# Last loop body of a mixture-of-experts kernel written out, with the last gate ahead of its predecessor's down

## The chip, the cores and the metric

The kernel runs on one core of one Trainium2 chip. The metric is the device time of one execution in microseconds; the median of three runs counts.

## What is computed

One inference step of a hybrid decoder with one layer: a mixing block (short convolution and a gated recurrence), then a mixture of experts over 320 tokens (256 new ones and 8 x 8 sampled ones), then a final norm. The change lies in the mixture of experts, where each token takes the best 4 of 32 experts:

```
for e in range(N_EXPERTS):                       # 32
    a = minimum(t @ w_gate[e] + b_gate[e], 7.0)
    u = clip(t @ w_up[e] + b_up[e], -7.0, 7.0)
    hid = (u + 1.0) * a * sigmoid(1.702 * a)
    y = y + combine[:, e:e+1] * (hid @ w_down[e] + b_down[e])
```

Every weight matrix is 1024 x 1024 in float32, 4 MB; 32 experts have 96 of them, 403 MB.

## The kernel before

**Slots.** In a round each expert takes up to 64 of its tokens. `gather(m)` picks their rows on TensorE with a matrix `P` of zeros and ones (the rows as three bfloat16 parts, L1299 and L1302), ScalarE copies them (`keep_rows`, L597), TensorE transposes them (`turn`, L1370) and VectorE writes the operand `xgT` (`gathered`, L962). `turn_gates` (L1364) makes the scatter matrix `PT`. After down, the result is split into three bfloat16 parts (`split_rows`: L625 and L627 on ScalarE, L980 and L983 on VectorE) and `scatter` (L1382) spreads them back over the tokens in three blocks; VectorE weighs each block and adds it to `x` (`add_rows`, L974).

**Products.** `product(mat, bank, lhs, e, it, j, between, operand)` computes one of gate (0), up (1), down (2): a bias row (L1391), then eight k steps of two halves (L1409; one half is two instructions in float32). After each second k it counts one slot as used (`wUsed`) and calls an entry of `between`.

**Ring.** Weights live in a ring of 16 slots of 1 MB, four matrices deep. SyncE issues the loads on one queue, each when the slots it overwrites are used. The loop's first bodies load whole matrices (L282); the last `FINE` = 2 bodies load halves of 2 MB (`load_half`, L287), and the last down ends in two pieces of 1 MB (`load_quarter`, L292). TensorE waits for the first half on `ringIn`, for the second on `lateIn` at k = 4, and for the last quarter of the last down on `endIn` at k = 6.

**Loop.** All engines run `Fori(0, BODIES)`: 8 bodies of 4 experts, 12 matrices each. For expert e TensorE does: gate of e, with the three scatters of e-1 between its k steps; up of e; `gather` of e+1; transposes of hidden (L1451), which ScalarE copies (L621) for down; `turn_gates` and `turn` of e+1; down of e. VectorE turns gate's result into `gt` (L1011, L1014, with ScalarE's sigmoid L617) and up's into `hid` (L1016, L1020). GpSimd writes `eh`, the row that selects expert e+1's bias (`pick`, L429). In the last expert the same instructions prepare expert 32, which doesn't exist. After the loop the last rows are scattered (L1479), added (L1047), normed (L637, L644, L1042) and stored.

All later rounds, for experts with more than 64 tokens, run only where there are any; here there are none.

Of the kernel before, what the change touches and what calls it, by code (L numbers as in the profile page):

```python
# [5 lines left out]
def hybrid_shortconv_hgrn2_moe_step(nc, A):  # L6
# [15 lines left out]
    E = 32  # L22
# [20 lines left out]
    FIRST = 4  # L43

# [34 lines left out]
    with ctx:  # L79
# [100 lines left out]
        endIn = sem("end_in")  # L180
# [70 lines left out]
        def credit(eng, *sems):  # L251
            for s in sems:
                eng.sem_inc(s, START)

# [24 lines left out]
        def _(sp):  # L279
# [64 lines left out]
            sp.sem_inc(endIn, 16)  # L344

            def body(first, it, halves=False, ends=False):
                for i in range(MPB):
                    s, e, m = (L_EXP + 4 * i) % NR, it * PER_BODY + i // 3, i % 3
                    used = lambda n: (first + 4 * (i - 4) + n) + it * (LPE * PER_BODY) + START
                    if halves:  # L350
                        sp.wait_ge(wUsed, used(2))
                        load_half(e, m, s, 0, ringIn[s])
                        if ends and i == MPB - 1:
                            sp.wait_ge(wUsed, used(3))
                            load_quarter(e, m, s, 2, lateIn[s // 4])
                            sp.wait_ge(wUsed, used(4))
# [11 lines left out]
                if not ends:  # L368
                    sp.sem_inc(endIn, 16)
# [27 lines left out]
        def _(pool):  # L397
# [34 lines left out]
            def one_round(r):  # L432
                pool.wait_ge(ehDone, r * (E + 1) + START)
                pool.wait_ge(wUsed, r * (LPE * E) + START)
                pick(slice(0, 1), 0)
                with pool.Fori(0, BODIES) as it:
                    for j in range(PER_BODY):
                        pool.wait_ge(wUsed, r * (LPE * E) + (it * (LPE * PER_BODY) + LPE * j) + START)
                        pick(bass.ds(it * PER_BODY + (j + 1), 1), (j + 1) % 2)

# [6 lines left out]
        def _(act):  # L447
# [142 lines left out]
            def one_round(r):  # L590
# [20 lines left out]
                with act.Fori(0, BODIES) as it:  # L611
                    for j in range(PER_BODY):
                        e = e0 + (it * PER_BODY + j)
                        m = p0 + (it * PER_BODY + (j + 1))
                        act.wait_ge(aDone, e + 1 + START)
                        act.wait_ge(hidDone, e + START)
                        act.activation(gs, ga, ACT.Sigmoid, scale=ALPHA).then_inc(sigDone, 1)  # L617
                        keep_rows(m)
                        act.wait_ge(hidTMM, e + 1 + START)
                        act.wait_ge(wUsed, e * LPE + START)  # L620
                        act.activation(hidT, ps[:, 4, :], ACT.Copy).then_inc(hidTOut, 1)  # L621
                        keep_slots(m, e * 3 + 3, (j + 1) % 2)
                        act.wait_ge(wUsed, e * LPE + LPE + START)
                        act.wait_ge(scatMM, e * 3 + 3 + START)
                        act.activation(ysb[0], ps[:, 2, :], ACT.Copy).then_inc(yHigh, 1)  # L625
                        act.wait_ge(yRest, e + 1 + START)
                        act.activation(ysb[1], yrest, ACT.Copy).then_inc(yMid, 1)  # L627
# [20 lines left out]
        def _(dve):  # L648
# [295 lines left out]
            def one_round(r):  # L944
# [22 lines left out]
                def add_rows(m0, e, par):  # L967

                    dve.wait_ge(gatesDone, m0 + START)
                    for b in range(3):  # L970
# [33 lines left out]
                with dve.Fori(0, BODIES) as it:  # L1004
                    for j in range(PER_BODY):
                        e = e0 + (it * PER_BODY + j)
                        m = p0 + (it * PER_BODY + (j + 1))
                        prepare(m, bass.ds(it * PER_BODY + (j + 1), 1))
                        add_rows(p0 + (it * PER_BODY + j), e, (j + 1) % 2)
                        dve.wait_ge(wUsed, e * LPE + 4 + START)  # L1010
                        TS(ga, ps[:, 0, :], LIMIT, None, ALU.min).then_inc(aDone, 1)  # L1011
                        dve.wait_ge(aDone, e + 1 + START)
                        dve.wait_ge(sigDone, e + 1 + START)
                        TT(gt, ga, gs, ALU.mult).then_inc(tDone, 1)  # L1014
                        dve.wait_ge(wUsed, e * LPE + 8 + START)
                        TS(gu, ps[:, 1, :], LIMIT, -LIMIT, ALU.min, ALU.max).then_inc(uDone, 1)  # L1016
                        dve.wait_ge(tDone, e + 1 + START)
                        dve.wait_ge(uDone, e + 1 + START)
                        dve.wait_ge(hidTMM, e + START)
                        STT(hid, gu, 1.0, gt, ALU.add, ALU.mult).then_inc(hidDone, 1)  # L1020
                        dve.wait_ge(accDone, e * 3 + 3 + START)
                        keep_gates(m, bass.ds(it * PER_BODY + (j + 1), 1), (j + 1) % 2)
                        gathered(m)
                        split_rows(e)
# [29 lines left out]
        def _(pe):  # L1054
# [292 lines left out]
            def one_round(r):  # L1347
                p0, e0 = r * (E + 1), r * E

                def gather(m):  # L1350

                    pe.wait_ge(prep, m + 1 + START)
                    pe.wait_ge(xgTOut, m + START)
                    if not isinstance(m, int):
# [31 lines left out]
                def product(mat, bank, lhs, e, it, j, between=(), operand=None):  # L1386
# [6 lines left out]
                    if operand:  # L1393
                        pe.wait_ge(*operand)
                    for k in range(KT):
                        n = LPE * j + 4 * mat + k // 2
                        s = (L_EXP + n) % NR
                        i = 3 * j + mat
# [6 lines left out]
                        if k == 6 and i == MPB - 1:  # L1405
                            pe.wait_ge(endIn, (r * BODIES + it) * 16 + 16)
# [21 lines left out]
                with pe.Fori(0, BODIES) as it:  # L1428
                    for j in range(PER_BODY):
                        e = e0 + (it * PER_BODY + j)  # L1430
                        m0 = p0 + (it * PER_BODY + j)
                        m = p0 + (it * PER_BODY + (j + 1))

                        def scatter_before(b, e=e, m0=m0, j=j):
                            if b == 0:
                                pe.wait_ge(yLow, e + START)
                                pe.wait_ge(yMid, e + START)
                                pe.wait_ge(gtOut, m0 + START)
                            scatter(b, e, (j + 1) % 2)

                        pe.wait_ge(ehDone, m + START)
                        pe.wait_ge(xgTOut, m + START)
                        pe.wait_ge(aDone, e + START)
                        product(0, 0, half_c(xgT), e, it, j, [lambda: None] + [lambda b=b: scatter_before(b) for b in range(3)])
                        pe.wait_ge(uDone, e + START)
                        product(1, 1, half_c(xgT), e, it, j)
                        gather(m)
                        pe.wait_ge(hidDone, e + 1 + START)
                        pe.wait_ge(hidTOut, e + START)
                        for c in range(4):  # L1450
                            ins = TR(ps[:, 4, 128 * c:128 * c + 128], fourth(hid, c), ident)  # L1451
                        ins.then_inc(hidTMM, 1)
                        turn_gates(m)
                        turn(m)
                        pe.wait_ge(yRest, e + START)
                        product(2, 2, half_c(hidT), e, it, j, operand=(hidTOut, e + 1 + START))
# [72 lines left out]
```

## Time and profile before

| | us |
|---|---|
| median of three runs | 1144.34 |
| lowest, highest | 1143.99, 1145.71 |
| the profiled execution | 1145.68 |
| its span, first to last instruction | 1143.9 |
| TensorE busy | 1107.1 (97%) |
| VectorE busy | 399.2 (35%) |
| ScalarE busy | 163.1 (14%) |
| mean DMA rate over the span | 378 GB/s |

The profile is of one execution, with times in microseconds from the span's start. Ends of matmuls are modelled, so that a busy TensorE isn't TensorE at its peak. "Idle before" an instruction is put down to what ended it. SPq, DVEq and the like are the queues in which an engine's instructions are issued. PE is TensorE's matmul, PEld its weight load, DVE VectorE, ACT ScalarE, POOL GpSimd, SP SyncE.

### The profile page before, as it was taken

The page shows a single profiled execution, that of the slowest core. Times are in us where ns is not written, and L with a number is a line of the kernel's source. Part 1 is how long each engine was busy: PE and PEld are TensorE (multiplying, and loading weights), DVE is VectorE, ACT ScalarE, POOL GpSimd, SP SyncE. Part 2 cuts the span into 40 slices and gives each one's busy share as a digit, 9 for nine tenths or more (in the row PEclk, how much of TensorE's full clock was granted, in tenths as well). Part 3 has the DMA queues.
Part 4 walks back from the last instruction along what each step waited for, and adds up shares of the span by engine and source line. Part 5 has one row for each costly group of instructions (what it writes and reads, how often), then busy time and mean ns, then how long its engine had stood idle before and what let it go on. Part 6 is the DMA issues. An engine that isn't in the chain of part 4 may idle for free.

```text
span 1143.9 us, 15163 instructions
## 1 busy us (share of the span) xinstructions
PE 1107.1 (97%) x6046; PEld 462.5 (40%) x6046; DVE 399.2 (35%) x711; ACT 163.1 (14%) x286; POOL 23.3 (2%) x51
## 2 busy tenths in 40 slices
PE   8999999999999999999999999999999999999996
PEld 5786764333333333333333333333333333333332
DVE  4155285633333333333332333322233332333333
ACT  3100114311111111111111011111111111111112
POOL 0002000000000000000000000000000000000000
PEclk9999999999999999999999999999999999999998
DMA  9970317799999999999999999999999999999993
GB/s 317 334 220 1 148 64 312 265 398 429 423 430 434 431 432 433 432 432 430 433 430 433 429 435 429 434 434 430 433 429 430 428 428 426 430 430 426 429 429 150
DMA packets 38990, 432.31 MB, mean 378 GB/s; under 512 B 2927, under 2 KB 18099, under 8 KB 22197
## 3 DMA queue, kind: packets, MB, share of 16 engines
q1 hardware_dynamic: 37312, 428.13, 89.9%
q0 software_dynamic: 848, 3.03, 0.7%
q10 hardware_dynamic: 805, 0.82, 0.2%
q8 instruction: 15, 0.25, 0.1%
q14 instruction: 10, 0.08, 0.0%
HBM read 428.26 MB, written 3.71 MB: 378 GB/s over the span
## 4 chain that ended last, share of the span: by engine, by line
PE 69%; DMA 28%; DVE 1%; ACT 0%; issue 0%; SPq 0%; DVEq 0%
PE ps L1409 39%; DMA ring<-in_w_gate 22%; PE ps L1117 9%; DMA ring<-in_w_up 6%; PE ps L1382 4%; PE ps L1234 3%; PE ps L1299 3%; PE ps L1391 2%; PE ps L1302 1%; PE ps L1370 1%; PE ps L1451 1%; PE ps L1107 1%; PE ps L1144 1%; PE ps L1364 1%; DMA consts<-in_consts 0%; PE ps L1111 0%
## 5 line engine op out<-in xcount | busy, mean ns | idle before, releaser
L1409 PE MATMUL ps<-ring,R 128*64 128x512 f32 x3072 | 691.4, 595 | 19.8 <-DMA ring<-in_w_gate 15.7
L1409 PEld LDWEIGHTS ps<-ring,R 128*64 128x64 f32 x3072 | 209.1, 137 | 421.1 <-issue 375.1
L974 DVE SCALAR_TENSOR_TENSOR x<-ps,gates,x 128x1024 f32<-128x1024 f32 (+1 forms) x96 | 106.2, 1106 | 136.9 <-PE ps L1382 136.9
L1117 PE MATMUL ps<-R,ring 128*128 128x320 f32 x384 | 107.3, 435 | 0.6 <-DVE R L687 0.6
L980 DVE TENSOR_TENSOR R<-ps,R 128x512 f32<-128x512 f32 x32 | 22.1, 692 | 228.9 <-ACT R L625 228.9
L1117 PEld LDWEIGHTS ps<-R,ring 128*128 128x128 f32 x384 | 71.8, 190 | 31.2 <-issue 1.8
L1382 PE MATMUL ps<-R 64*128 64x512 bf16 (+1 forms) x576 | 79.3, 381 | 0.0
L1016 DVE TENSOR_SCALAR R<-ps 128x512 f32<-128x512 f32 x32 | 22.1, 692 | 146.1 <-PE ps L1409 146.1
L617 ACT ACTIVATE R<-R 128x512 f32<-128x512 f32 x32 | 20.1, 630 | 310.4 <-DVE R L1011 310.4
L1382 PEld LDWEIGHTS ps<-R 64*128 64x128 bf16 (+1 forms) x576 | 21.5, 98 | 88.8 <-issue 56.0
L597 ACT ACTIVATE R<-ps 128x512 f32<-128x512 f32 x33 | 19.7, 597 | 239.8 <-PE ps L1302 239.8
L625 ACT ACTIVATE R<-ps 128x512 bf16<-128x512 f32 x32 | 19.1, 597 | 228.1 <-PE ps L1409 228.1
L1299 PE MATMUL ps<-R,P 128*64 128x512 bf16 x396 | 50.4, 388 | 0.0
L962 DVE TENSOR_TENSOR R<-ps,par 128x512 f32<-128x512 f32 x33 | 22.8, 692 | 66.8 <-PE ps L1370 66.8
L1391 PE MATMUL ps<-R,eh 128*64 128x512 bf16 x192 | 38.9, 402 | 0.4 <-DVE R L962 0.4
L1299 PEld LDWEIGHTS ps<-R,P 128*64 128x64 bf16 x396 | 22.2, 109 | 34.4 <-issue 19.3
L1234 PE MATMUL ps<-ring,R 128*128 128x512 f32 (+1 forms) x96 | 35.9, 598 | 0.0
L1014 DVE TENSOR_TENSOR R<-R 128x512 f32<-128x512 f32 x32 | 22.2, 693 | 25.1 <-ACT R L617 25.1
L983 DVE TENSOR_TENSOR R<-R 128x512 bf16<-128x512 f32 x32 | 22.2, 693 | 22.3 <-ACT R L627 22.3
L1302 PE MATMUL ps<-R,P 128*64 128x256 bf16 x396 | 28.0, 275 | 0.0
L429 POOL CAST eh<-consts 128x64 bf16 (+1 forms) x33 | 7.8, 238 | 884.5 <-PE ps L1409 884.5
L1302 PEld LDWEIGHTS ps<-R,P 128*64 128x64 bf16 x396 | 22.0, 108 | 8.1 <-issue 0.4
(227 smaller groups left out, 590.1 us busy)
## 6 DMA issues: line engine op xcount, KB each, us to landing
ring<-in_w_gate SPq DMA_DIRECT2D x22, 4096.0 KB, 27.8
ring<-in_w_up SPq DMA_DIRECT2D x21, 4096.0 KB, 29.4
ring<-in_w_down SPq DMA_DIRECT2D x21, 4096.0 KB, 31.2
ring<-in_w_down SPq DMA_DIRECT2D x21, 2048.0 KB, 33.7
ring<-in_w_gate SPq DMA_DIRECT2D x20, 2048.0 KB, 32.5
ring<-in_w_up SPq DMA_DIRECT2D x20, 2048.0 KB, 34.1
ring<-in_w_in SPq DMA_DIRECT2D x14, 1024.0 KB, 12.9
ring<-in_w_out SPq DMA_DIRECT2D x4, 1024.0 KB, 9.6
```

The lines of the kernel that those rows point to most:

```text
L962: TT(xgT.rearrange("p (c a s) -> p c a s", c=4, a=2), ps[:, 3, :].rearrange("p (c a s) -> p c a s", c=4, a=2), par[:, NG:NG + 8].rearrange ...
L974: STT(xb[b], rows, gates[:, par, b:b + 1], xb[b], ALU.mult, ALU.add).then_inc(accDone, 1)
L980: TT(yrest, ps[:, 2, :], ysb[0], ALU.subtract).then_inc(yRest, 1)
L983: TT(ysb[2], yrest, ysb[1], ALU.subtract).then_inc(yLow, 1)
L1014: TT(gt, ga, gs, ALU.mult).then_inc(tDone, 1)
L1117: ins = MM(ps[:, n % 2, 0:NT], slot_k(L, 256)[:, k, 128 * half:128 * half + 128], hT[:, k, :], start=(k == 0), stop=(k == KT - 1))
L1234: ins = MM(dst, mixT[:, k, t0:t0 + n], w[:, 512 * half:512 * half + 512], start=(k == 0), stop=(k == KT - 1))
L1299: ins = MM(in_fours(to), P[:, b, 0:SLOTS], half_of(h2p[:, part, b, :], half), start=(b == 0 and part == 0), stop=False)
L1302: ins = MM(in_fours(to[:, 256 * at:256 * at + 256]), P[:, 2 + at, 0:SLOTS], half_of(h2p[:, part, 2, 0:HALF], half), start=False, stop=(par ...
L1382: ins = MM(to, PT[64 * half:64 * half + 64, par, t0:t0 + n], ysb[part][64 * half:64 * half + 64, :], start=(part == 0), stop=(part == 2))
L1391: MM(shape(ps[64 * half:64 * half + 64, bank, :]), eh[:, j % 2, :], cols(bias3[:, mat, :], half), start=True, stop=False)
L1409: ins = MM(shape(ps[64 * half:64 * half + 64, bank, :]), lhs(k), cols(w, half), start=False, stop=(k == KT - 1))
```

## The change

The first seven bodies stay in the loop (`ahead(r)`); the eighth is written out for round 0, on all engines. In it, experts 28 and 29 run as before. The order of the last four matrices becomes gate of 31, down of 30, up of 31, down of 31, and the loads follow that order (`LAST_ORDER`). Down of 30 therefore comes after gate of 31, and the three scatters of expert 30's rows lie in up of 31 in place of gate of 31. Nothing is gathered, turned or picked for an expert 32; semaphores that would have counted it are raised. Two matmuls without use (`fill`) stand before the transposes of the last hidden and two after. Up of 31 is loaded as a half and two pieces of 1 MB, each with a wait of its own, as down of 31 already was. The loop no longer waits for `endIn` in each body. The diff is cut to what matters; the helpers that it only moves into functions are left out.

```diff
+    G31, D30, U31, D31 = range(MPB - 4, MPB)
+    LAST_ORDER = {G31: (E - 1, 0), D30: (E - 2, 2), U31: (E - 1, 1), D31: (E - 1, 2)}
...
-        endIn = sem("end_in")
+        endIn = {U31: sem("up31_end_in"), D31: sem("down31_end_in")}
...
+        def ahead(r):
+
+            return BODIES - 1 if isinstance(r, int) else BODIES
...
                     s, e, m = (L_EXP + 4 * i) % NR, it * PER_BODY + i // 3, i % 3
+                    if ends and i in LAST_ORDER:
+                        e, m = LAST_ORDER[i]
...
-                        if ends and i == MPB - 1:
+                        if ends and i in endIn:
                             sp.wait_ge(wUsed, used(3))
                             load_quarter(e, m, s, 2, lateIn[s // 4])
                             sp.wait_ge(wUsed, used(4))
-                            load_quarter(e, m, s, 3, endIn)
+                            load_quarter(e, m, s, 3, endIn[i])
...
+                    sigmoid(E - 2)
+                    keep_rows(E - 1)
+                    keep_hidden(E - 2, LPE * (E - 2))
+                    keep_slots(E - 1, 3 * (E - 1), 1)
+                    sigmoid(E - 1)
+                    split_rows(E - 2, LPE * E - 8)
+                    keep_hidden(E - 1, LPE * E - 8)
+                    split_rows(E - 1, LPE * E)
...
+                    activate_gate(E - 1, LPE * E - 12)
+                    split_rows(E - 2)
+                    add_rows(E - 1, E - 1, 0, (0, 1))
+                    activate_up(E - 1, LPE * E - 4)
+                    add_rows(E - 1, E - 1, 0, (2,))
+                    split_rows(E - 1)
...
-                        if k == 6 and i == MPB - 1:
-                            pe.wait_ge(endIn, (r * BODIES + it) * 16 + 16)
+                        if k == 6 and isinstance(it, int) and it == BODIES - 1 and i in endIn:
+                            pe.wait_ge(endIn[i], 16)
...
+                def fill(n):
+
+                    for _ in range(n):
+                        MM(ps[:, 3, :].rearrange("p (n t) -> p n t", n=4), onesb[:], onesb[:].unsqueeze(1).broadcast_to([128, 4, 128]),
+                           start=True, stop=True)
...
+                    for j in range(PER_BODY - 1):
+                        e = E - PER_BODY + j
+                        gate_and_up(e, e + 1, it, j)
+                        if e < E - 2:
+                            down(e, it, j)
+                    e, j = E - 1, PER_BODY - 1
+                    pe.wait_ge(ehDone, e + 1 + START)
+                    pe.wait_ge(xgTOut, e + 1 + START)
+                    pe.wait_ge(aDone, e + START)
+                    product(0, 0, half_c(xgT), e, it, j, i=G31)
+                    pe.wait_ge(yRest, e - 1 + START)
+                    product(2, 2, half_c(hidT), e - 1, it, j - 1, operand=(hidTOut, e + START), i=D30)
+                    pe.wait_ge(uDone, e + START)
+                    product(1, 1, half_c(xgT), e, it, j, [lambda: None] + [lambda b=b: scatter_before(b, e, e, j) for b in range(3)], i=U31)
+                    fill(2)
+                    turn_hidden(e)
+                    fill(2)
+                    pe.wait_ge(yRest, e + START)
+                    product(2, 2, half_c(hidT), e, it, j, operand=(hidTOut, e + 1 + START), i=D31)
+                    for done in (xgMM, gtMM, xgTMM):
+                        pe.sem_inc(done, 1)
```

## Rows read from the trace of the kernel before

**Rows 1.** Granted clock in 40 slices; DMA queues from 350 to 1060 us (packets, MB, share).

```profile
PEclk9999999999999999999999999999999999999998
...
q1 hardware_dynamic: 13049, 305.88, 100.4%
```

**Rows 2.** Chain of waits, 990 to 1144: start us, us, what.

```profile
1078.37 0.76 PE ps L1382 x6
1079.12 1.89 PE ps L1409 x8
...
1081.03 34.51 DMA ring<-in_w_up
...
1115.59 3.65 PE ps L1409 x16
1119.24 1.36 PE ps L1299 x12
...
1121.28 0.68 PE ps L1451 x4
...
1122.87 0.34 PE ps L1391 x2
1123.21 6.89 PE ps L1409 x32
```

**Rows 3.** Order of time, TensorE: start, us, line, what, idle before and its releaser.

```profile
1105.80 1.94 PE L1409 MATMUL ps<-ring,R 128*64 128x512 f32 x8 [0.49 <-DMA ring<-in_w_gate]
```

**Rows 4.** Issues of up and down of expert 31 (ns, first and last start), their landings.

```profile
L287 SPq DMA_DIRECT2D ring<-in_w_up x2: 327/328/328, 1075.2 to 1081.0; - x2
...
DMA to landing us min/median/max: 34.5/35.0/35.4
...
L292 SPq DMA_DIRECT2D ring<-in_w_down x2: 327/327/327, 1088.2 to 1089.9; - x2
...
DMA to landing us min/median/max: 34.7/34.9/35.4
```

**Rows 5.** Order of time, VectorE, ScalarE and the transposes around the last products.

```profile
1093.55 0.69 DVE L962 TENSOR_TENSOR R<-ps,par 128x512 f32<-128x512 f32 x1 [2.07 <-PE ps L1370]
...
1120.08 0.69 DVE L1020 SCALAR_TENSOR_TENSOR R<-R 128x512 f32<-128x512 f32 x1
...
1121.21 0.75 PE L1451 MATMUL ps<-consts,R 128*128 128x128 f32 x4
...
1122.07 0.60 ACT L621 ACTIVATE R<-ps 128x512 f32<-128x512 f32 x1 [0.15 <-PE ps L1451]
...
1132.14 0.69 DVE L983 TENSOR_TENSOR R<-R 128x512 bf16<-128x512 f32 x1 [0.70 <-ACT R L627]
```

**Rows 6.** Chain of waits, 208 to 300: five filling matmuls, and a product's first half.

```profile
213.37 1.19 PE ps L1312 x5
...
218.26 3.43 PE ps L1409 x16
```

**Rows 7.** Code queue q8 at 287 to 290 and 311 to 314; loads issued then, landings.

```profile
q8 instruction: 1, 0.02, 2.3%
...
L287 SPq DMA_DIRECT2D ring<-in_w_gate x1: 328/328/328, 273.5 to 273.5; - x1
L287 SPq DMA_DIRECT2D ring<-in_w_up x1: 328/328/328, 277.2 to 277.2; - x1
...
DMA to landing us min/median/max: 13.8/14.6/15.4
...
q8 instruction: 1, 0.02, 2.0%
...
L287 SPq DMA_DIRECT2D ring<-in_w_down x1: 327/327/327, 290.4 to 290.4; - x1
...
L282 SPq DMA_DIRECT2D ring<-in_w_gate x1: 352/352/352, 301.4 to 301.4; - x1
...
DMA to landing us min/median/max: 15.6/16.2/16.9
```

More of the change, by code:

```diff
@@ L435, in one_round @@
                 pick(slice(0, 1), 0)
-                with pool.Fori(0, BODIES) as it:
+                with pool.Fori(0, ahead(r)) as it:
                     for j in range(PER_BODY):
@@ new lines, in expert @@
+                def expert(e, m, j):
+                    sigmoid(e)
+                    keep_rows(m)
+                    keep_hidden(e, e * LPE)
+                    keep_slots(m, e * 3 + 3, (j + 1) % 2)
+                    split_rows(e, e * LPE + LPE)
+                with act.Fori(0, ahead(r)) as it:
+                    for j in range(PER_BODY):
+                        expert(e0 + (it * PER_BODY + j), p0 + (it * PER_BODY + (j + 1)), j)
+                if isinstance(r, int):
+                    for j in range(PER_BODY - 2):
+                        expert(E - PER_BODY + j, E - PER_BODY + j + 1, j)
+                    sigmoid(E - 2)
[6 more added lines that the diff above has]
+                    split_rows(E - 1, LPE * E)
+                    act.sem_inc(xgOut, 1)
+                    act.sem_inc(gtOut, 1)
@@ L965, in gathered, with add_rows @@
                        ALU.mult).then_inc(xgTOut, 1)
-                def add_rows(m0, e, par):
+                def add_rows(m0, e, par, blocks=range(3)):
                     dve.wait_ge(gatesDone, m0 + START)
-                    for b in range(3):
+                    for b in blocks:
                         dve.wait_ge(scatMM, e * 3 + (b + 1) + START)
@@ new lines, in activate_gate, with activate_up @@
+                def activate_gate(e, used):
+                    dve.wait_ge(wUsed, used + START)
+                    TS(ga, ps[:, 0, :], LIMIT, None, ALU.min).then_inc(aDone, 1)
+                    dve.wait_ge(aDone, e + 1 + START)
+                    dve.wait_ge(sigDone, e + 1 + START)
+                    TT(gt, ga, gs, ALU.mult).then_inc(tDone, 1)
+                def activate_up(e, used):
+                    dve.wait_ge(wUsed, used + START)
+                    TS(gu, ps[:, 1, :], LIMIT, -LIMIT, ALU.min, ALU.max).then_inc(uDone, 1)
+                    dve.wait_ge(tDone, e + 1 + START)
+                    dve.wait_ge(uDone, e + 1 + START)
+                    dve.wait_ge(hidTMM, e + START)
+                    STT(hid, gu, 1.0, gt, ALU.add, ALU.mult).then_inc(hidDone, 1)
@@ new lines, in expert @@
+                def expert(e, m, j, col):
+                    prepare(m, col)
+                    add_rows(m - 1, e, (j + 1) % 2)
+                    activate_gate(e, e * LPE + 4)
+                    activate_up(e, e * LPE + 8)
+                    dve.wait_ge(accDone, e * 3 + 3 + START)
+                    keep_gates(m, col, (j + 1) % 2)
+                    gathered(m)
+                with dve.Fori(0, ahead(r)) as it:
+                    for j in range(PER_BODY):
+                        expert(e0 + (it * PER_BODY + j), p0 + (it * PER_BODY + (j + 1)), j, bass.ds(it * PER_BODY + (j + 1), 1))
+                        split_rows(e0 + (it * PER_BODY + j))
@@ new lines, in one_round @@
+                if isinstance(r, int):
+                    for j in range(PER_BODY - 1):
+                        e = E - PER_BODY + j
+                        expert(e, e + 1, j, slice(e + 1, e + 2))
+                        if e < E - 2:
+                            split_rows(e)
+                    activate_gate(E - 1, LPE * E - 12)
[4 more added lines that the diff above has]
+                    split_rows(E - 1)
+                    dve.sem_inc(prep, 1)
+                    dve.sem_inc(gatesDone, 1)
+                    dve.sem_inc(xgTOut, 1)
@@ L1427, in one_round @@
                 pe.wait_ge(zeroed, 1)
-                with pe.Fori(0, BODIES) as it:
-                    for j in range(PER_BODY):
[L1430 to L1456, printed above, removed]
@@ new lines, in scatter_before, with turn_hidden @@
+                def scatter_before(b, e, m0, j):
+                    if b == 0:
+                        pe.wait_ge(yLow, e + START)
+                        pe.wait_ge(yMid, e + START)
+                        pe.wait_ge(gtOut, m0 + START)
+                    scatter(b, e, (j + 1) % 2)
+                def turn_hidden(e):
+                    pe.wait_ge(hidDone, e + 1 + START)
+                    pe.wait_ge(hidTOut, e + START)
+                    for c in range(4):
+                        ins = TR(ps[:, 4, 128 * c:128 * c + 128], fourth(hid, c), ident)
+                    ins.then_inc(hidTMM, 1)
@@ new lines, in gate_and_up @@
+                def gate_and_up(e, m, it, j):
+                    pe.wait_ge(ehDone, m + START)
+                    pe.wait_ge(xgTOut, m + START)
+                    pe.wait_ge(aDone, e + START)
+                    product(0, 0, half_c(xgT), e, it, j, [lambda: None] + [lambda b=b: scatter_before(b, e, m - 1, j) for b in range(3)])
+                    pe.wait_ge(uDone, e + START)
+                    product(1, 1, half_c(xgT), e, it, j)
+                    gather(m)
+                    turn_hidden(e)
+                    turn_gates(m)
+                    turn(m)
```

80 lines of the change are left out of this document (37 added, 43 removed).

## Prediction, written before the changed kernel ran

> **What bounds the kernel now.** First the slices of the page and the queue view of 350 to 1060 us: one queue, q1, keeps the sixteen DMA engines at 100.4% of their time, and nothing else runs beside it; TensorE's granted clock is full (9) in every slice but the last [rows 1]. So the weight stream sets when each expert's matrices are there. Then the chain of waits, read from its end backwards. It leaves the stream at 1115.54, where the second half of w_up of expert 31 lands after 34.51 us in the queue, and from there on it is TensorE alone: the rest of up, two gather rows, the turning of hidden and two more turns, a bias row, and 6.89 us of the last down, to 1130.10 [rows 2]. The last down is fed in time: its two 1 MB pieces land at 1088.2 + 34.7 = 1122.9 and 1089.9 + 35.4 = 1125.3 [rows 4], and its last quarter isn't read before 1123.21 + 0.75 x 6.89 = 1128.4. The end is thus the stream up to U31 (up of 31) plus 14.6 us of TensorE, plus the final scatter and norm, some 13.8 us to the span's end at 1143.9, which the change leaves alone.
>
> I write G, U, D for gate, up, down of an expert, h0 and h1 for the halves of a load.
>
> **What doesn't move.** The first seven bodies run the same instructions in the same order. In the last body the loads keep their places in the ring and in the queue: place 8 now brings G31, place 9 D30, place 10 U31, place 11 D31. Their issues wait for slots used by places 4 to 7, which run in the old order. The queue is 34 to 35 us deep, so landings stay. U31 was issued at 1075.2 and 1081.0, with 35.4 and 34.5 us to landing [rows 4]: h0 lands at 1110.6, h1 at 1115.5. Halves are therefore 4.9 us apart. Cut in two, h1 gives one quarter at about 1113.1 and the other still at 1115.5. SP gets one more wait and one more issue; behind them stand only D31's loads, which have 3 us to spare (1125.3 against 1128.4). In the trace 1 MB pieces follow each other by 2.4 us, the same bytes per us as the halves, so the cut costs 0. The Trainium skill (DMA: Bandwidth & Descriptors, Bandwidth) gives 341 GB/s for a single 1 MB transfer against 425 for a large one; by that an estimate is 0.6 us for each of the two pieces. The rows of D31's pieces don't agree with it, since they queue behind others.
>
> **The new order, step by step** (times of the span of before).
> - G31 starts after up of 30 and its turns. It needs xgT, which DVE writes until 1093.55 + 0.69 = 1094.24 [rows 5], where before D30 started without it. G31 with bias then ends near 1094.3 + 0.34 + 6.89 = 1101.5; the scatters that used to sit in G31 are no longer in it. Its h1 landed long before (place 8, 9.8 us before place 9's 1105.8).
> - D30: bias 0.34, first half 3.4, to 1105.3; then it waits for place 9's h1, which lands at about 1105.76, as G31's k = 4 did (started 1105.80) [rows 3], and ends at 1105.8 + 3.65 = 1109.5.
> - U31: the bias goes first, then h0 is awaited until 1110.6. TensorE stands for 0.9 us there. So the lateness of G31 by 0.8 us and the removed scatters (3 x 0.76) both vanish in this wait: their value is nothing. From 1110.7: first four k 3.65, scatter 0.76, two k 1.89, scatter 0.76, two k 1.89 [rows 2] gives 1110.7 + 8.95 = 1119.6. The quarters (1113.1, 1115.5) are there before they are read (1115.1, 1117.8). D30's rows for the scatter are split 2.7 us after its end, as D31's are now (1130.10 to 1132.83) [rows 5], by 1112.2, ahead of the first scatter at 1114.3. Before, U31 ended at 1115.59 + 3.65 = 1119.24. This part is **0.4 us later**, because two scatters now lie between h0's landing and the end of up. Without the cut it would be 1115.6 + 1.94 + 0.76 + 1.89 = 1120.2, so the two pieces are worth 0.6 us.
> - U31's end to D31's first matmul. Before: gather 2.04 (1119.24 to 1121.28), the turns of hidden, gates and rows 1.59, of which hidden's are 0.68, bias 0.34, together 3.97 [rows 2]. The DVE work (0.05 after up's end, two instructions, hidden ready at 1120.77, 1.53 after up's end [rows 5]) was hidden beneath the gather. It comes out now: scatter 0.76 and two fills at 1.19 / 5 = 0.24 [rows 6] last 1.24, less than 1.53 + 0.06. Then the transposes, 0.86 from their start to the start of ACT's copy and 0.60 for that [rows 5], and 0.05 to TensorE: 1.59 + 0.86 + 0.60 + 0.05 = 3.10. TensorE's own queue (0.7 turn, 0.48 fill, 0.34 bias) takes 1.52 beside ACT's 1.51: level. This part is **0.9 us shorter**: of 2.95 us of work (2.04 + 0.91) that is no longer there, two thirds only uncover a wait that it hid.
> - D31 itself 6.89, at most 0.2 more where it starts from a wait (16 matmuls take 3.65 from a wait, 3.43 in a run) [rows 2, 6].
>
> Sum: + 0.4 - 0.9 + 0.1 = **- 0.4 us**.
>
> **What the trace of before doesn't show** is the price of straight code in a saturated stream. TensorE's loop is fetched once: from 218 to 314 us five blocks of 16 KB come over q8, one in about 23 us, and until 1060 none [rows 1, 7]. Written out, the last body must be fetched too: some 5 blocks between 1012 and 1130, of which 4 or 5 before U31's h0 lands. One takes 2.3% of 16 engines in 3 us, 1.1 us of one engine. A load has landed when its slowest engine is done. At 287 to 290 the landings went from 273.5 + 13.8 = 287.3 to 277.2 + 15.4 = 292.6, 5.3 us where 4.9 is usual: 0.4 lost. At 311 to 314 they went from 290.4 + 16.9 = 307.3 to 301.4 + 15.6 = 317.0, 9.7 us for 4 MB where 2 x 4.9 is usual: nothing lost [rows 7]. So a block costs 0 to 0.4 us and 4.5 of them 0 to 1.8. A gain is excluded: they only add bytes. I take 0.07 (1.1 us spread over 16 engines), 0.3 in all, since the later of the two rows lost nothing. The smaller blocks of the other engines lie inside the same bounds. The Trainium skill (Runtime: NRT & Kernel Launch, Instruction fetch mechanics) has an engine stream its code in 16 KiB blocks over a DMA queue of its own, mostly hidden, and warns of taken branches instead. By that rule the written-out body is free, and the sum would be -0.4. The rows agree on block size and queue and are split on "hidden". A stall of TensorE itself at the loop's exit of up to 1 us would be given back before U31, in the 0.9 us wait and the one before D30's second half.
>
> Forecast: - 0.4 + 0.3 = - 0.1 us. The profiled run of 1145.68 us with span 1143.9 would have span 1143.8; it lies 1.3 us above the median of three runs, 1144.34, whose spread is 1.7 us. Against the median: **1144.2 us**. What a measurement of this kernel can tell from no change is about 0.2%, 2.3 us.
>
> **The rivals.**
> - *Up is held by its last quarter, not by its first half.* If TensorE had its first six k and two scatters behind it when the last quarter lands, up would end at 1115.6 + 1.94 = 1117.5 and all would be 2.1 us earlier: -2.2, 1142.1 us. That needs h0 at 1108.6, 2 us before the rows put it. For: two pieces are cut for that. Against: the issue and landing row [rows 4]. 5%.
> - *The code blocks hold the stream* (the slower side). Price 0.4 x 4.5 = 1.8 against the 0.4 gained: +1.4, 1145.7 us, and with 0.6 a block +2.3. It decides from 0.09 us a block on. For: the landing at 292.6. Against: the one at 317.0. 20%.
> - *The clock falls before D31.* The granted clock was full across all waits of this stage [rows 1]; the new longest wait is 0.9 us at U31. If the level fell to half before D31, its 6.9 us would double: 1151 us. 3%.
> - *Only the order changes, and nothing of the tail*: the same time within 0.4 us as my forecast; it isn't told apart by time, only by the trace.
>
> **How the numbers follow.** The forecast has 72%, with its own range 1143.3 to 1145.0. The range for 8 in 10 takes in the code blocks and most of the early case: 1142.4 to 1146.2. Faster by over 0.2% (below 1142.05) is half of the first rival and a remainder, 4%. Slower by over 0.2% (above 1146.6) is the clock and the far end of the blocks, 7%. The rest, 89%, is within 0.2%.
>
> **What would show it.** Right: G31's first matmul 0.8 us after the turn of the rows; TensorE waiting for w_up of 31 for about 0.9 us; the chain entering TensorE at h0 of U31 (before: at h1), some 19 us ahead of the end of D31; hidden's transposes waiting 0.3 us for DVE; D31 starting 22.7 after 1100. Four or five q8 packets between 1012 and 1110, and landings 4.9 us apart. Wrong: landings after a q8 packet 5.3 us apart, U31's h0 after 1111.5; or U31 ending by 1118, or a granted clock below full before 1130.

## The result, and the profile after

The changed kernel takes 1147.71 us in the median of 17 runs (1145.69 to 1149.28), the kernel before 1144.92 (17 runs, 1143.32 to 1147.80): a ratio of 1.0023, 95% interval 1.0016 to 1.0029, so 2.6 us slower (1.8 to 3.3). The profiled execution took 1147.40 us with a span of 1145.6; that of before 1145.68 with 1143.9.

The first lines are of the page of the changed kernel: granted clock in 40 slices, and the two queues that carry code. Before, q8 had 15 packets in the whole execution, and 20 now; q14 had 10, and 12 now. Writing out TensorE's code alone adds to q8 and not to q14 (e1), writing out VectorE's alone adds to q14 and not to q8 (e2).

```profile
PEclk9999999999999999999999999999999999999997
...
q8 instruction: 20, 0.33, 0.1%
q14 instruction: 12, 0.09, 0.0%
```

The chain of waits of the changed kernel, 990 to 1146 us (start us, us, what), answers to [rows 2]:

```profile
1075.18 35.42 DMA ring<-in_w_up
...
1110.64 3.65 PE ps L1473 x16
1114.29 0.75 PE ps L1446 x6
...
1117.67 1.89 PE ps L1473 x8
...
1119.58 0.70 DVE R L1054
...
1120.37 0.70 DVE R L1058
...
1121.12 0.75 PE ps L1505 x4
...
1122.30 0.34 PE ps L1455 x2
1122.63 7.03 PE ps L1473 x32
...
1129.68 0.61 ACT R L639
...
1131.70 0.04 DVE R L1022
...
1132.30 0.06 DVEq L268
1132.36 0.15 DVE posm L1092
1132.52 2.69 issue
1135.21 0.02 DVEq L1109
...
1135.28 3.15 DVE x L1111 x3
```

Read it down to the last down: up's first half enters at 1110.64, up ends at 1119.56, the last down starts at 1122.63 and ends at 1129.66, 0.45 us before that of the kernel before. Then come lines that the chain of before does not have. VectorE executes a branch (L268, over the rounds that don't run) at 1132.30 and for 2.69 us after its last small instruction nothing is issued. The first add (L1111) starts 5.62 us after the end of down; before, it was 1133.55 - 1130.11 = 3.44. So the profile says - 0.45 + 2.18 = + 1.7, which is the 1.7 us between the spans. TensorE and VectorE of the kernel before at the same place, in order of time:

```profile
1130.87 0.94 PE L1479 MATMUL ps<-R 64*128 64x512 bf16 x6 [0.79 <-ACT R L625]
...
1133.55 3.13 DVE L1047 SCALAR_TENSOR_TENSOR x<-ps,gates,x 128x1024 f32<-128x1024 f32 x3 [0.59 <-PE ps L1479]
```

The same of the changed kernel, with the idle time before each row and its releaser; the second row is the first one up to 1134.3 us alone:

```profile
1132.03 3.62 PE L1581 MATMUL ps<-R 64*128 64x512 bf16 x18 [2.39 <-DVEq L1088]
1132.03 2.63 PE L1581 MATMUL ps<-R 64*128 64x512 bf16 x14 [2.39 <-DVEq L1088]
...
1135.28 3.13 DVE L1111 SCALAR_TENSOR_TENSOR x<-ps,gates,x 128x1024 f32<-128x1024 f32 x3 [2.76 <-PE ps L1581]
```

TensorE's final scatter starts 2.4 us after down, not 0.8, and what it waited for is L1088: `dve.sem_inc(xgTOut, 1)`, one of the increments by hand for expert 32, which stand behind VectorE's last split. After that wait the scatter also runs at the lower clock; columns of these rows are busy us (and count) of TensorE, weight loads, VectorE, ScalarE and GpSimd, then the granted clock, the DMA engines' share and GB/s:

```profile
1130.00:1132.00 2.00, 0.00 (x0) 0.00 (x1) 0.99 (x2) 0.91 (x2) 0.00 (x0) 1.00 0.05 12
1132.00:1134.00 2.00, 1.97 (x12) 0.49 (x12) 0.52 (x2) 1.49 (x2) 0.00 (x0) 0.83 0.01 4
1134.00:1136.00 2.00, 1.65 (x8) 0.26 (x6) 0.72 (x1) 0.00 (x0) 0.00 (x0) 0.50 0.00 0
```

So the tail held three suspects: VectorE's branch, the late increments, and the half clock (0.50 is 1.2 GHz) that followed TensorE's wait. Two paths lead to the first add, and the longer one counts. One is VectorE's, held here until 1135.21. The other is the scatter: in every trace in which the chain goes through 14 of its matmuls in one run, the add starts 0.1 us after the fourteenth. Here these 14 took 2.63 us and were done at 1134.66, so that VectorE's branch cost about 0.5 us beyond what the late and slowed scatter would have cost by itself.

The medians are 2.8 us apart (2.6 by the ratio) and the two profiled executions 1.7. Of that 1.1, 0.8 lies on the side of the kernel before, whose profiled execution is above its own median.

### The profile page after: what moved, and what is told of

The parts are those of the page before. It is cut to its first block, busy times and chain, and to the rows that moved or that the text cites. A ratio compares the mean times of both kernels' runs of the same rounds, so it can differ in the third digit from the quotient of the medians.

```text
span 1145.6 us, 15013 instructions
## 1 busy us (share of the span) xinstructions
PE 1107.8 (97%) x6019; PEld 462.3 (40%) x6019; DVE 397.8 (35%) x706; ACT 162.1 (14%) x284; POOL 23.1 (2%) x50
## 4 chain that ended last, share of the span: by engine, by line
PE 72%; DMA 25%; DVE 2%; issue 1%; ACT 0%; DVEq 0%; SPq 0%
PE ps L1473 41%; DMA ring<-in_w_gate 16%; PE ps L1181 9%; DMA ring<-in_w_up 9%; PE ps L1446 4%; PE ps L1298 3%; PE ps L1363 3%; PE ps L1455 2%; PE ps L1366 1%; PE ps L1505 1%; PE ps L1434 1%; PE ps L1171 1%; PE ps L1208 1%; PE ps L1428 1%; PE ps L1124 0%
## 5 line engine op out<-in xcount | busy, mean ns | idle before, releaser
L609 ACT ACTIVATE R<-ps 128x512 f32<-128x512 f32 x32 | 19.1, 598 | 231.7 <-PE ps L1366 231.7
L639 ACT ACTIVATE R<-ps 128x512 bf16<-128x512 f32 x32 | 19.1, 597 | 227.7 <-PE ps L1473 227.7
```

## The experiments

Each kernel is measured against the kernel before on the same chip. Three figures are read from each trace: the *lead*, from the landing of up's first half to the first add; the *gap*, from the end of the last down to the first add; and the *slip*, the time from TensorE's restart at the second half of gate 28 to up 31's first half, less what it is without extra code blocks (93.0; 97.9 where up's second half is what is awaited).

### Where does the loss come from: writing out TensorE's code, or VectorE's?

**e1_pe_out**: the old order, the last body written out on TensorE alone.

```diff
-                with pe.Fori(0, BODIES) as it:
-                    (body)
+                    with pe.Fori(0, BODIES - 1) as it:
+                        whole_body(it)
+                    whole_body(BODIES - 1)
```

> The kernel before, with the last loop body written out on TensorE alone, in the old order; all other engines keep their loop. It isolates what fetching five more 16 KB blocks of TensorE's code costs. Theory 'VectorE stalls at its branch' (VectorE, after its last piece of work, jumps over the code of the rounds that don't run and waits 2.7 us for code): VectorE's code is untouched here, so its first add after the final scatter starts 0.1 us after TensorE, as before, and the span is 1143.9, +0.0. Rival 'the code blocks hold the weight stream': landings slip by up to 0.4 us at each block, up of expert 31 lands late by 0.5 to 1.8 us and the time is that much longer, in the median if not in the profiled run. Blocks on q8 between 1012 and 1130: five in both.

Measured: ratio 1.0001 (0.9992 to 1.0010), gap 3.45 as before. The profiled execution is 1145.7 long, and its whole excess lies in the stream. Chain of waits of e1_pe_out: 

```profile
1117.39 3.65 PE ps L1409 x16
...
1125.02 6.89 PE ps L1409 x32
...
1135.36 3.15 DVE x L1047 x3
```

It restarted at gate 28's second half at 1018.03, so up's second half came 99.4 us later, where before it is 1115.59 - 1017.67 = 97.9: a slip of 1.4 us in this execution. The timing, +0.1 us with 1.1 us to either side, doesn't settle how often. Writing out TensorE's code costs nothing in the tail.

**e2_dve_out**: the same on VectorE alone, TensorE and the others in their loop.

> The kernel before, with the last loop body written out on VectorE alone, in the old order; TensorE and the rest keep their loop. Theory 'VectorE stalls at its branch': the branch over the unused rounds comes at about 1132.9 and the code behind it isn't there, so the first add after the final scatter starts at about 1135.7 instead of 1133.55: +2.2 us, span 1146.1. Rival 'code blocks in the stream': VectorE's code is a few 8 KB blocks, +0.0 to 0.2. Rival 'late increments' (TensorE's final scatter waits for a semaphore that VectorE raises after its split): doesn't exist in this kernel, +0.0.

Measured: ratio 1.0016 (1.0005 to 1.0027), +1.8 us; gap 5.30. The chain of e2_dve_out after down:

```profile
1133.05 0.21 DVE posm L1039
1133.25 2.36 issue
...
1135.69 3.15 DVE x L1058 x3
```

The stall of 2.4 us appears in a kernel whose order, loads and TensorE code are those of before. This is the experiment that names the cause: VectorE's code, written out, costs 1.9 us at its branch. The granted clock was full until 1136 and the increments by hand don't exist here, so neither of the other two suspects is needed. The slip of 0.7 in this trace lies beside it.

### Repairing the tail, one cause at a time

**e4_branch_early**: the changed kernel, VectorE's last split moved into both arms of its branch, so that it jumps while it waits for down; increments still behind the split. VectorE's own waits for the increments by hand are left out of the first round.

```diff
-                    split_rows(E - 1)
+                    last_split.append(lambda: split_rows(E - 1))
...
-            further_rounds(dve, one_round, rounds=rounds[0])
+            with dve.If(rounds[0] > 1):
+                last_split[0]()
+                (increments, the further rounds)
+            with dve.Else():
+                last_split[0]()
+                (increments)
```

> The changed kernel with only the branch taken early; the increments still come after the split of the last down. It prices the two causes apart. Theory: the final scatter starts late as in the changed kernel (about 1132.0), but VectorE is at its wait in time, so the first add starts when the first block is scattered, about 1134.1: 1.2 us under the changed kernel's 1135.28, span 1144.4. Rival 'the branch is no stall, VectorE waits for TensorE': the first add stays at 1135.2.

Measured: gap 4.63 (down ends 1129.42, first add 1134.06), 1.0 less than in the changed kernel; ratio 1.0017 (1.0008 to 1.0027). The first add is where I had put it. TensorE and its chain, then the stretch with its clock (columns as above):

```profile
1131.80 2.68 PE L1597 MATMUL ps<-R 64*128 64x512 bf16 x18 [2.40 <-DVEq L1114]
...
1131.80 2.15 PE ps L1597 x14
...
1132.00:1134.00 2.00, 2.00 (x16) 0.44 (x12) 0.15 (x1) 1.40 (x2) 0.00 (x0) 1.00 0.00 0
```

TensorE waited 2.40 us, as long as in the changed kernel, and yet its clock stayed full: 14 matmuls in 2.15 us against 2.63. So only half of the 1.0 us is the branch; the other 0.5 is the clock, which this repair doesn't touch. In e10, which differs from the changed kernel in its fills alone, the clock stood at 0.50 from 1134 on, and the same 14 matmuls took 3.45. What decides whether the clock falls in such a wait is open.

Code moved with the branch: two blocks of 8 KB come over q14 between 1122 and 1126 here, none in the changed kernel. From 1131 on it is one here and three there.

**e9_incs_only**: its counterpart, only the increments moved ahead of the split, on VectorE and ScalarE.

```diff
-                    split_rows(E - 1)
                     dve.sem_inc(prep, 1)
                     dve.sem_inc(gatesDone, 1)
                     dve.sem_inc(xgTOut, 1)
+                    split_rows(E - 1)
```

> The changed kernel with only the stand-in increments of VectorE and ScalarE moved ahead of the last split; VectorE's branch stays behind the split. Counterpart of e4_branch_early. Theory 'VectorE's branch stall decides in the changed kernel': TensorE's final scatter starts 0.8 to 1.5 us after the last down's end instead of 2.4, but the first add still comes 5.2 to 5.6 us after that end (5.6 in the changed kernel, 3.4 before), since VectorE has no code until then: at most 0.4 us gained. Rival 'the increments decide': the first add comes 3.5 us after the end. One look.

Measured in one execution (1146.92 us): gap 5.26, so 0.36 gained. The scatter is done early and VectorE isn't there. TensorE and then the chain of e9_incs_only:

```profile
1130.36 0.94 PE L1581 MATMUL ps<-R 64*128 64x512 bf16 x6 [0.93 <-ACT R L639]
1131.51 1.81 PE L1581 MATMUL ps<-R 64*128 64x512 bf16 x12 [0.21 <-ACT R L641]
...
1132.30 2.34 issue
...
1134.71 3.14 DVE x L1111 x3
```

**e3_both_early**: VectorE's branch and VectorE's increments, both early.

> The changed kernel with two repairs on VectorE. The three increments that stand in for expert 32 come before the split of the last down, and the branch over the unused rounds is taken before that split, while VectorE waits for the last down anyway (the split stands in both arms of the branch). Theory 'stall at the branch plus late increments': TensorE's final scatter starts 1.2 us after the last down's end minus 0.4 (as before, 0.8 behind it, about 1130.5), the first add at 1133.1, span 1143.4, 2.2 us under the changed kernel and 0.4 under the one before (ratio 0.9996 if the stream costs nothing, 1.0005 if the blocks cost 1 us in the median). Rival 'the loss is in the stream': the span falls by less than 0.5 us from the changed kernel's.

Measured: span 1143.3, first add 1133.00, both as forecast, and for the wrong reason: in this execution up's first half was there 1.1 us earlier than in the changed kernel (1109.54), and the gap is 4.44, not 3.4. The ratio is 1.0008 (0.9999 to 1.0017). TensorE waited on, this time for ScalarE's increments:

```profile
1130.30 3.59 PE L1592 MATMUL ps<-R 64*128 64x512 bf16 x18 [1.76 <-ACTq L666]
```

I had overlooked `act.sem_inc(gtOut, 1)` behind ScalarE's split. Half of the 1.0 us that is left is again the clock: 0.91 and then 0.50 in the stretches of 2 us from 1130, and 14 matmuls in 2.62 us.

**e5_all_early**: ScalarE's increments early as well.

> The changed kernel with every repair of its tail: VectorE's and ScalarE's stand-in increments ahead of the last split, and VectorE's branch ahead of it. With VectorE's two repairs alone (e3_both_early) the first add after the final scatter still stood 4.4 us behind the end of the last down, against 3.4 in the kernel before, since TensorE waited until ScalarE had raised its own increments. Theory 'three causes in the tail': that gap is 3.4 to 3.5 us now, and the time is 2.2 us under the changed kernel: -0.4 from the new order, +0 to +1.6 from code blocks in the stream, so a ratio of 1.0000 to 1.0010 to the kernel before. Rival 'something else in the order': the gap stays at 4.4.

Measured: gap 3.62, against 5.62; the tail's loss is gone but for 0.2. Ratio 1.0007 (0.9998 to 1.0016), +0.8 us, with a slip of 1.0 in the trace. Chain of e5_all_early:

```profile
1131.67 0.75 issue
1132.42 2.15 PE ps L1592 x14
```

The clock was full. The branch alone gives 1.0 (0.5 of it the clock), the increments alone 0.4, both give 2.0: the two waits lie side by side, and the longer one counts. At the full clock both repairs are needed; how much of the changed kernel's median is the clock, no run prices.

### What do code blocks do to the stream?

**e7_pe_out_two**: e1 with two bodies written out.

```diff
-                    with pe.Fori(0, BODIES - 1) as it:
+                    with pe.Fori(0, BODIES - 2) as it:
                         whole_body(it)
+                    whole_body(BODIES - 2)
                     whole_body(BODIES - 1)
```

> The suspected cost doubled: as e1_pe_out, but the last two bodies are written out on TensorE, so some ten code blocks come during the last 235 us instead of five in 117. Measure: the landing of the first gate half of body 6 to that of the last up half, which without blocks is a fixed number of steps of 4.9 us. Theory 'a block delays one of sixteen engines by about 1.5 us, and the landings only if that engine is the last one': the landings slip by 0 to 3 us in steps, on average twice what e1_pe_out has (there 1.4 in the profiled run), median +0.5 to +2 us over the kernel before. Rival 'code blocks are free': landings 4.9 apart throughout, ratio 1.000.

Measured: ratio 1.0012 (1.0002 to 1.0021), +1.4 us, gap 3.44. In the trace the last body slips by 1.2. Body 6's first gate half lands at 893.8 and the next body's at 1012.7: 118.9 us apart, where the kernel before has 117.5 (895.2 to 1012.7), so 1.4 more. The interval excludes zero, if barely, so two bodies of code in the stream have a price; that of one body isn't told from zero by the clock (e1). The other timings of kernels with TensorE's code written out hold other changes too.

The clearest step is in e4_branch_early. Two loads there were issued at 1000.0 and 1007.4, and took 35.4 and 34.4 us to land (issues: duration ns, first and last start; then min/median/max to landing), with one block of code between 1035 and 1040 us on q8:

```profile
L293 SPq DMA_DIRECT2D ring<-in_w_down x1: 328/328/328, 1000.0 to 1000.0; - x1
L293 SPq DMA_DIRECT2D ring<-in_w_gate x1: 328/328/328, 1007.4 to 1007.4; - x1
...
DMA to landing us min/median/max: 34.4/34.9/35.4
...
q8 instruction: 1, 0.02, 1.4%
```

The landings are 1035.4 and 1041.8, 6.4 apart where 4.9 is usual: 1.5 us lost to one block of 16 KB, which itself took 1.1 us of one engine (1.4% of sixteen in 5 us), and not made up later (slip 1.6 at up 31). The other blocks of that body cost nothing. In e1, e5, e8 and e11 the largest step too stands at the block of 1038 to 1041: 1.1, 1.0, 1.5 and 0.7 us. In the changed kernel that block, at 1038.7, cost nothing. Slips of the last body in all profiled kernels in which TensorE's code is written out: after 0.0, e1 1.4, e3 0.0, e4 1.6, e5 1.0, e7 1.2, e8 1.5, e9 0.7, e10 0.0 (its restart at gate 28 is itself 0.7 late), e11 0.7; mean 0.8. Where it isn't: e2 0.7, e6 0.0, e12 0.3, before 0.0; mean 0.2. The slips of e2 and e12 stand at a block of 8 KB on q14 at 1094.4, which the kernel before fetches too, at 1094.8, without a loss: the old code wasn't quite free either. The profiled execution of the changed kernel is one without a slip, which fits that it shows 1.7 us and the medians more. What decides which block costs something (its place among the sixteen engines would fit, if a load waits for the slowest, as the prediction has it) isn't shown: the traces here don't name the engine of a packet.

### What the parts that were meant to help are worth

**e6_up_pieces**: the kernel before with nothing but up's second half in two 1 MB pieces.

```diff
-        endIn = sem("end_in")
+        endIn = {MPB - 2: sem("up_end_in"), MPB - 1: sem("end_in")}
...
-                        if ends and i == MPB - 1:
+                        if ends and i in endIn:
...
-                        if k == 6 and i == MPB - 1:
-                            pe.wait_ge(endIn, (r * BODIES + it) * 16 + 16)
+                        if k == 6 and i in endIn:
+                            pe.wait_ge(endIn[i], (r * BODIES + it) * 16 + 16)
```

> One part of the change alone: the kernel before, its loop and its order untouched, with the last up loaded as a half and two 1 MB pieces. Theory (my working): before, up's second half is awaited until 1115.54 and ends at 1119.24. With the pieces nothing is awaited: up starts its matmuls at 1111.4 and ends 6.87 later at 1118.3, 0.95 us earlier, all of it kept to the end: span 1142.95, ratio 0.9992. In the changed kernel the same pieces are worth 0.6. Rival 'pieces of 1 MB slow the stream': the last piece lands later than 4.9 us after the half, and nothing is gained.

Measured: lead 22.0 against 22.9 (1133.55 - 1110.65), where 0.95 had been forecast; up's first half lands at 1110.94 here. Chain of e6_up_pieces:

```profile
1111.77 6.87 PE ps L1411 x32
1118.63 1.35 PE ps L1301 x12
...
1132.95 3.15 DVE x L1049 x3
```

Up runs its 32 instructions without a wait, where before it stood until 1115.54 for its second half [rows 2]. The ratio is 0.9999 (0.9989 to 1.0010).

**e12_up_pieces_again**: the same kernel once more.

> e6_up_pieces once more, for a narrower interval: in its trace the first add stands 22.0 us after the landing of up's first half, against 22.95 before, with landings unchanged; the ratio of its first timing was 0.9999 with an interval of 0.2%. Theory: -0.9 us, 0.9992. Rival: nothing gained, 1.0000. Beside it in the same call e11 tells which of the two is faster.

Measured: 1144.70 against 1145.64, ratio 0.9993 (0.9982 to 1.0004), lead 22.0. Both intervals hold 0.9992 and both hold 1. It is the only version whose median lies below that of the kernel before measured beside it, and it does so in both timings. But that it beats the kernel before is shown by the traces only, not by the time.

**e8_old_order**: all repairs, but down of 30, gate of 31 with its scatters, up of 31, in the old order.

```diff
-    LAST_ORDER = {G31: (E - 1, 0), D30: (E - 2, 2), U31: (E - 1, 1), D31: (E - 1, 2)}
+    LAST_ORDER = {}
...
-                    product(0, 0, half_c(xgT), e, it, j, i=G31)
-                    product(2, 2, half_c(hidT), e - 1, it, j - 1, operand=(hidTOut, e + START), i=D30)
-                    product(1, 1, half_c(xgT), e, it, j, [lambda: None] + [... 3 scatters], i=U31)
+                    product(0, 0, half_c(xgT), e, it, j, [lambda: None] + [... 3 scatters])
+                    product(1, 1, half_c(xgT), e, it, j)
```

> The changed kernel with all three repairs and the order taken back: down of 30, gate of 31 with the scatters in it, up of 31 in pieces, down of 31; nothing for an expert 32. It tells what the new order itself is worth. Theory (the scatters behind up's first half cost more than the order saves): up ends at 1118.3 of the span of before instead of 1119.6, the last down starts 3.1 us later at 1121.4 and ends at 1128.3, 1.35 us before that of the changed kernel and 1.8 before that of the kernel before, counted from the landing of up's first half; with blocks in the stream ratio 0.9985 to 1.0000. Rival 'the order is what brings the gain': the last down ends no earlier than in the changed kernel.

Measured: the last down ends 17.8 us after up's first half has landed (1112.6 to 1130.42), against 19.1 in the changed kernel (1110.6 to 1129.66): the new order costs 1.3 us, by the two scatters (1.5 us) that it puts behind up's first half. But the gap is 4.87, and most of the gain is lost there; ratio 1.0000 (0.9991 to 1.0010). Chain and TensorE of e8_old_order:

```profile
1131.05 1.37 issue
1132.42 2.77 PE ps L1581 x14
...
1132.42 3.75 PE L1581 MATMUL ps<-R 64*128 64x512 bf16 x18 [2.02 <-issue]
```

Neither VectorE nor ScalarE is named now: TensorE had nothing issued. It started 5.05 us after the last weight piece had landed (1127.37). In e5 this is 5.5, in e6 4.8, in e12 4.9, and in the kernel before, where ScalarE releases it, 5.5. So there is a second floor under the tail. The likely reading, which e11 tests: TensorE's sequencer gets past the wait for the last piece, then reads the count of rounds, branches and waits for code. The clock adds to it: it stood at 0.90 and then 0.50 from 1132 on, and the 14 matmuls took 0.6 us more than the 2.15 of e5.

**e11_pe_branch_early**: e8 with TensorE's branch ahead of the last up, and up and down in both arms.

> As e8_old_order (old order, pieces, nothing for expert 32, VectorE's branch and all increments early), and TensorE's branch over the unused rounds taken before the last up, which with the last down stands in both arms. In e8 the last down ended 1.3 us earlier than in the changed kernel, counted from the landing of up's first half (17.9 against 19.1), but TensorE's final scatter began only 2.0 us after it, with a 16 KB block of its code arriving in between, and about 5 us after the last weight piece. Theory 'TensorE too stands at its branch for code, which it asks for only once the last piece has landed': the scatter now starts 0.8 us after the end, the first add 3.4 to 3.5 after it, 21.4 after the landing of up's first half (22.95 before, 24.7 changed): -1.6 us against before, +1.0 for code blocks in the stream, ratio 0.9990 to 1.0005. Rival 'ScalarE or VectorE holds the scatter': the 2.0 us stay.

Measured: ratio 1.0067 (1.0050 to 1.0083), 7.7 us slower. The gap is 3.43, so the cause of e8's late scatter was right. The branch was not hidden, though. Chain of e11_pe_branch_early:

```profile
1114.23 6.22 issue
1120.45 0.64 PE ps L1458 x2
1121.09 8.68 PE ps L1476 x29
```

TensorE stood for 6.2 us, and the granted clock fell to half behind it: 0.97 in 1114 to 1118, 0.50 in 1118 to 1122, so that up took 8.9 us and not 6.9. Blocks of 16 KB come over q8 at 1117.9 and 1123.5 and none after that, where e8 has one at 1129.8, just before down ends, and one at 1132.9. I had counted on the queued matmuls to cover the branch. It stands behind scatters that wait for VectorE, which is the likely reason that they didn't; no run moves it.

**e10_no_fill**: the changed kernel without its four filling matmuls.

```diff
-                    fill(2)
                     turn_hidden(e)
-                    fill(2)
```

> The changed kernel without its four filling matmuls around the last transposes. Theory: they lie in waits of 0.3 and 0.7 us; the last down starts at the same 12.0 us after the landing of up's first half, and the granted clock stays full. Rival 'the clock falls without them': the last down takes more than its 7.0 us. One look.

Measured in one execution (1149.38 us): down starts 11.9 us after up's first half (1112.22 to 1124.14), 12.0 with them, and takes 7.1 at the full clock. The fills do nothing for down. The gap is 5.91, 0.3 more, with 14 matmuls of the scatter in 3.45 us; one execution doesn't tell whether the fills' absence brought the clock down sooner.

## Why the prediction was wrong

- **G31, D30 and up, step by step: right.** G31 started late (bias at 1094.28; forecast 1094.3), D30 waited until 1105.74 (1105.8), up ran from 1110.64 (1110.7) to 1119.56 (1119.6), down from 1122.63 (1122.7), and ended 0.45 us before that of before (0.4). TensorE waited 1.0 us for up's first half (0.9) and 0.28 for hidden (0.3): the wait that the gather had covered came out as written.
- **"The final scatter and norm, some 13.8 us, which the change leaves alone": wrong, and the failed step.** It is 15.9 us. I stopped the walk at the last matmul of down and didn't ask what every engine must have issued by then. Two things moved there. VectorE's three increments and ScalarE's two for expert 32, which before were early side effects of real work (the instruction of `gathered(32)` was over at 1123.6, 6.5 us before the end of down), stood behind the last split: a semaphore raised by hand is a step of the change with a place in its engine's order. And VectorE stood at its last branch, as it does with nothing but its own last body written out (e2). Repaired alone they give 0.4 and 1.0, together 2.0 (e9, e4, e5). In these sums the clock of the final scatter has a part of its own, 0.5 us between the changed kernel and e4; the prediction's walk hadn't asked for it there either.
- **Code blocks in the stream: right mechanism, mis-sized term.** I had 0.3 us and 0 to 1.8 as bounds. The traces have 0.8 in the mean, from 0 to 1.6, in steps of up to 1.5 for one block, where the nearest rows [rows 7] had led me to an upper end of 0.4 a block. Averaging one engine's delay over sixteen was the mistake: the steps are 0 for most blocks and up to 1.5 for one. Less the 0.2 of the kernels without such blocks, the mean slip is 0.6, twice the term. With the profile's 1.7 that makes 2.3 us, within the interval of 1.8 to 3.3.
- **TensorE's stall at the loop's exit: there was none.** It started the gate of 28 at 1012.78, and at 1012.77 before; the prediction had allowed up to 1 us, to be given back before up.
- **The rivals.** Up held by its last quarter didn't come (first half at 1110.6). The slower side was named, with the code blocks as its cause, and by code blocks alone the changed kernel would have stayed inside the range. The clock rival had the mechanism but not the place: it fell around the wait of 2.4 us before the final scatter, not before down, and in e4 it didn't fall in the same wait.
- The Trainium skill (Runtime: NRT & Kernel Launch, Instruction fetch mechanics) says that a taken branch whose target isn't in the engine's window of code forces a fetch before execution goes on. The prediction cites that rule and then applies it to the loop's exit, where nothing was lost. The traces agree with it at the branch over the unused rounds: 2.4 to 2.7 us on VectorE (e2, after), 6.2 on TensorE (e11), and the blocks on q14 that move with VectorE's branch (e4). That VectorE had the code in the kernel before because its last body had been fetched seven bodies earlier, while here it is read as it goes, is the likely reading, and no run separates it.

## What to carry to other kernels

A body written out isn't free at its end: look for the next branch on each engine, and put it where the engine waits anyway, and read in a trace that it does wait there: on VectorE that won up to 1.0 us (e4), on TensorE it lost 7.7 (e11). Where semaphores are raised by hand for work that is left out, raise them where that work would have, not at the end. And ask of a new order what lies between the landing that bounds it and the work that follows: here two scatters behind up's first half cost 1.3 us against the old order (e8), and of 2.95 us of work for an expert that isn't there only 0.9 came off, since it had been hiding a wait.

## What was not expected of the hardware

One block of 16 KB of code put back all further landings of a saturated stream by 1.5 us (e4), others by nothing. At a jump over unused code VectorE stood for 2.3 to 2.7 us (e9, e2, the changed kernel), and TensorE for 6.2 (e11), with the reading of the count in it. In e5, e6, e8 and e12, with a branch between, TensorE's final scatter started 4.8 to 5.5 us after the landing that its sequencer waited for last. After 2.4 us without a matmul the granted clock stood at 0.83 and then 0.50 in the next two stretches of 2 us in the changed kernel, and at 1.00 in both in e4.
